# A decoder layer with 32 experts on one core: the second modulation fused in row form, its row tiles handled one by one, and a fourth split buffer for the first expert

## The reference, cut to what matters

```
mod = silu(c) @ w_ada + b_ada ; shift1, scale1, g1, shift2, scale2, g2 = split(mod)
mixed = (sigmoid(ga) * y_ret + sigmoid(gb) * y_fox) @ w_o
x = LN(1.189 * x + (1 + g1) * mixed) * ln1_w + ln1_b
h = x * (1 + scale2) + shift2
group = top1(softmax(h @ w_rg + b_rg)) ; experts = top2(in that group, h @ w_re + b_re)
y = sum over the 2 chosen experts of gate * ((silu(a) * u) @ w_e_out[e]),  a, u = split(h @ w_e_in[e])
x = LN(1.189 * x + (1 + g2) * y) * ln2_w + ln2_b
```

## Time and profile before

| | us |
|---|---|
| median of three runs (lowest, highest) | 1232.74 (1231.88, 1235.53) |
| the profiled execution, its own time | 1232.76 |
| its span, first to last instruction | 1230.9 |
| busy: PE, DVE, ACT, POOL | 1035.5, 877.7, 636.7, 260.7 |
| 566 to 607 us: PE busy, DVE busy, mean granted clock | 23.1, 27.7, 0.83 |
| 607 to 629 us: the same | 13.7, 17.8, 0.50 |
| 629 to 647 us: the same | 4.0, 10.3, 0.50 |
| 647 to 708 us: the same | 47.2, 48.1, 0.88 |

### The profile page before, as it was taken

How to read it: one execution, slowest core, us unless ns; L and a number is a source line. 1 busy time by engine, 2 the same in 40 slices (tenths; PEclk the granted TensorE clock), 3 DMA queues, 4 the chain that set the end, 5 groups by cost and what they waited for, 6 DMA issues and landing times.

```text
span 1230.9 us, 13075 instructions
## 1 busy us (share of the span) xinstructions
PE 1035.5 (84%) x4460; PEld 720.0 (58%) x4460; DVE 877.7 (71%) x944; ACT 636.7 (52%) x642; POOL 260.7 (21%) x192
## 2 busy tenths in 40 slices
PE   4698969899999999999247899999999999999950
PEld 2365647587777676677235556656665566556630
DVE  3868643396433444556766989999999999999947
ACT  3644414133323344523104677778777777777732
POOL 0240871010001000002807622111111122122210
PEclk8898988999999999999658999999999999999975
DMA  9777552255123324247126799999999999999923
GB/s 330 246 257 250 178 189 105 84 189 194 53 78 121 120 77 153 96 157 235 55 101 201 279 399 388 389 393 391 396 392 394 402 396 394 393 393 397 394 95 107
DMA packets 102666, 303.40 MB, mean 246 GB/s; under 512 B 10740, under 2 KB 10788, under 8 KB 102118
## 3 DMA queue, kind: packets, MB, share of 16 engines
q1 hardware_dynamic: 92888, 282.75, 61.7%
q0 software_dynamic: 9744, 20.19, 5.2%
HBM read 299.97 MB, written 14.73 MB: 256 GB/s over the span
## 4 chain that ended last, share of the span: by engine, by line
PE 60%; DVE 13%; POOL 10%; DMA 7%; ACT 5%; issue 4%; SPq 0%; ACTq 0%; POOLq 0%; DVEq 0%
PE banks L2025 10%; PE banks L1711 8%; PE banks L1722 8%; PE banks L2033 8%; PE banks L2021 7%; PE banks L1713 5%; DVE w_lo L1586 5%; ACT w_hi L972 4%; PE banks L2014 2%; DVE w_lo L1060 2%; DMA mod_sample<-scratch_mod 1%; PE banks L2040 1%; DMA w_raw<-in_w_ada 1%; DMA x_item<-scratch_h,slot_token 1%; POOL x L785 1%
## 5 line engine op out<-in xcount | busy, mean ns | idle before, releaser
L1586 DVE TENSOR_TENSOR w_lo<-w_raw,w_hi 128x2048 fp32r<-128x2048 f32 x157 | 360.2, 2311 | 38.5 <-ACT w_hi L972 38.5
L972 ACT ACTIVATE w_hi<-w_raw 128x2048 fp32r<-128x2048 f32 x157 | 295.6, 1903 | 0.9 <-PE banks L2025 0.7
L1060 DVE TENSOR_TENSOR w_lo<-w_raw,w_hi 128x2048 fp32r<-128x2048 f32 x72 | 165.7, 2319 | 79.6 <-ACT w_hi L811 79.4
L811 ACT ACTIVATE w_hi<-w_raw 128x2048 fp32r<-128x2048 f32 x72 | 136.8, 1910 | 140.3 <-PE banks L1722 110.4
L2025 PE MATMUL banks<-w_lo,xT_item 128*128 128x512 f32 x512 | 148.7, 412 | 47.1 <-DVE w_lo L1586 47.1
L2021 PE MATMUL banks<-w_hi,xT_item 128*128 128x512 f32 x512 | 157.4, 429 | 4.6 <-ACT w_hi L972 3.0
L2025 PEld LDWEIGHTS banks<-w_lo,xT_item 128*128 128x128 f32 x512 | 92.2, 190 | 92.9 <-DVE w_lo L1586 75.1
L1711 PE MATMUL banks<-w_hi,h_hi 128*128 128x512 f32 x384 | 142.6, 412 | 3.1 <-DVE gate_b L1098 1.4
L2021 PEld LDWEIGHTS banks<-w_hi,xT_item 128*128 128x128 f32 x512 | 94.7, 191 | 39.7 <-issue 14.4
L742 POOL DMA_INDIRECT scratch_y<-y_item,slot_row x29 | 63.9, 2204 | 226.0 <-DVE y_item L1610 209.0
L2033 PE MATMUL banks<-w_raw,hiddenT 128*128 128x512 f32 x248 | 111.4, 592 | 0.0
(11 more groups left out here) (427 smaller groups left out, 1488.5 us busy)
## 6 DMA issues: line engine op xcount, KB each, us to landing
w_raw<-in_w_e_in SPq DMA_DIRECT2D x128, 1024.0 KB, 7.2
w_raw<-in_w_e_out SPq DMA_DIRECT2D x64, 1024.0 KB, 5.8
w_raw<-in_w_in SPq DMA_DIRECT2D x32, 1024.0 KB, 8.9
w_raw<-in_w_ada SPq DMA_DIRECT2D x24, 1024.0 KB, 7.8
bias_rows<-in_b_in SPq DMA_DIRECT2D x16, 256.0 KB, 4.3
w_raw<-in_w_ret_proj SPq DMA_DIRECT2D x4, 1024.0 KB, 10.6
w_raw<-in_w_fox_proj SPq DMA_DIRECT2D x4, 1024.0 KB, 11.9
w_raw<-in_w_o SPq DMA_DIRECT2D x4, 1024.0 KB, 5.0
```

Of the source, the lines that this page charges most:

```text
L811: nc.scalar.activation(whi[n % NSPL][:], raw[n % NRAW][:], ACT.Copy).then_inc(hi_done, 1)
L972: nc.scalar.activation(whi[ss][:], raw[j][:], ACT.Copy).then_inc(hi_done, 1)
L1060: V.tensor_tensor(wlo[n % NSPL][:], raw[n % NRAW][:], whi[n % NSPL][:].bitcast(F32), ALU.subtract).then_inc(lo_done, 1)
L1586: V.tensor_tensor(wlo[ss][:], raw[j][:], whi[ss][:].bitcast(F32), ALU.subtract).then_inc(lo_done, 1)
```

## The change

Five things are changed.

1. The modulation. `ada6` and `ada7` (shift2) now stay in `mod_rows`. When `ada8` and `ada9` (scale2) are evacuated, three more instructions on 2 x 512 values form (1 + scale2) * ln1_b + shift2 and (1 + scale2) * ln1_w right there. Two broadcast loads of ln1's rows (`ln_rows`) are issued ahead. POOL writes the finished shift row to `scratch_mod` after `ada9`, and waits for that write (`t2_out`) before the second `rotary`, since this writes over `mod_rows`. The eight POOL instructions and two loads later on are gone.
2. LN1 and h. Each row tile has its own variance, deviation, and two instructions for h straight from x; the three are placed among the instructions of the second `evac_wo`. x itself stays unnormalised until the tail. ACT instead of DVE copies the lower 64 rows (`low_rows`). PE computes a tile's logits right after its transposes. The router's weights are loaded earlier.
3. The routing chain has one instruction for three in five places, and `lo(N0 + 2)` is moved behind the last one-hot product. The token index is released ahead of the row index.
4. Item 0's fourth piece has its own buffers (`xhi`, `xlo`) and is split on ACT between the copies of h, and on DVE after the routing chain. ACT and DVE take item 1's first piece in its old place.
5. POOL's six instructions on x among the first items are gone. DVE does LN1's affine part with six instructions of 1024 columns ahead of the tail's first combination. The four tail loads, now six, stand behind the third gather.

The core of the diff:

```diff
+    xhi = at("w_hi_first", [P, 4, 512], F32R, 65536)
+    xlo = at("w_lo_first", [P, 4, 512], F32R, 90112)
+    FIRST_FREE = (N0 + 2, N0 + 3, N0 + 1, E0 + 1, E0 + 2)
@@ gpsimd
-            pool.dma_start(scratch["mod"][:, 512 * (j - 4):512 * (j - 3)], mrow[:, j % 2, :]).then_inc(mod_out[j % 2], 16)
+            if j not in SHIFT2:
+                pool.dma_start(scratch["mod"][:, 512 * (j - 4):512 * (j - 3)], mrow[:, j % 2, :]).then_inc(mod_out[j % 2], 16)
+            if j == 9:
+                pool.dma_start(scratch["mod"][:, D:2 * D], mod[:, D:2 * D]).then_inc(t2_out, 16)
+                pool.wait_ge(t2_out, 16)
             if 8 <= j <= 10:
                 rotary(j - 8)
...
-        pool.wait_ge(m2_in, 32)
-        pool.wait_ge(ln_in, 32)
-        for m2, rows in ((m2p, P), (m2s, DEC)):
...
-        pool.wait_ge(evacuated, CI["wo0"] + 1)
+        pool.wait_ge(used, SI[("wo1", 0)] + 1)
...
         gather_item(1)
-
+        gather_item(2)
...
-        for t in range(3):
-            rows = P if t < 2 else DEC
-            st(nc.gpsimd.tensor_tensor(x1[0:rows, t, :], x1[0:rows, t, :], l1w[0:rows, :], ALU.mult))
-            st.settle()
-            st(nc.gpsimd.tensor_tensor(x1[0:rows, t, :], x1[0:rows, t, :], l1b[0:rows, :], ALU.add), x1_ready)
@@ vector
+        def modulated(t):
+            rows = P if t < 2 else DEC
+            xt, ht = x1[0:rows, t, :], h2[0:rows, t, :]
+            m2 = m2p if t < 2 else m2s
+            dve.wait_ge(ln_std, t + 1)
+            st(V.reciprocal(mv[:, t, 1:2], mv[:, t, 1:2]))
+            if t == 0:
+                dve.wait_ge(m2_in, 32)
+            st(V.scalar_tensor_tensor(ht, xt, mv[0:rows, t, 0:1], m2[0:rows, 1, :], ALU.subtract, ALU.mult))
+            st.settle()
+            st(V.scalar_tensor_tensor(ht, ht, mv[0:rows, t, 1:2], m2[0:rows, 0, :], ALU.mult, ALU.add), h2_ready)
...
+            st(V.scalar_tensor_tensor(srow[:], rows, 1.0, l1r[:, 1, half], ALU.add, ALU.mult))
+            st(V.scalar_tensor_tensor(rows, rows, 1.0, l1r[:, 0, half], ALU.add, ALU.mult))
+            st.settle()
+            st(V.tensor_tensor(shift, shift, srow[:], ALU.add), evacuated)
...
+        dve.wait_ge(used, N0)
+        dve.wait_ge(hi_done, N0 + 4)
+        V.tensor_tensor(xlo[:], raw[(N0 + 3) % NRAW][:], xhi[:].bitcast(F32), ALU.subtract).then_inc(lo_done, 1)
         x_low(0)
-        lo(N0 + 3)
+        item_lo(1, 0)
...
-        dve.wait_ge(tail_in, 64)
-        dve.wait_ge(x1_ready, 3)
+        dve.wait_ge(tail_in, 96)
+        for t in range(3):
+            rows = P if t < 2 else DEC
+            xt = x1[0:rows, t, :]
+            st(V.scalar_tensor_tensor(xt, xt, mv[0:rows, t, 0:1], l1w[0:rows, :], ALU.subtract, ALU.mult))
+            st.settle()
+            st(V.scalar_tensor_tensor(xt, xt, mv[0:rows, t, 1:2], l1b[0:rows, :], ALU.mult, ALU.add))
@@ tensor
-            if t:
-                logits(t - 1)
-        logits(2)
+            logits(t)
```

More of the change, by code:

```diff
@@ L1001, in item @@
         def item(e, second):
-            item_hi(e, 0)
+            if not (isinstance(e, int) and e == 1):
+                item_hi(e, 0)
             silu(e - 1)
@@ L1526, in _ @@
         st.settle()
[L1527 to L1528 removed]
+        st(V.tensor_tensor(oht6, oh6, exc[:, :].unsqueeze(1).to_broadcast([P, 6, NE]), ALU.mult))
         st.settle()
@@ L1617, in item_steps @@
         def item_steps(e, second, third):
-            item_lo(e, 0)
+            if not (isinstance(e, int) and e == 1):
+                item_lo(e, 0)
             hidden(e - 1)
@@ L2020, in product @@
                 for half in range(2):
-                    mm(bank[b0 + half], X[:, k0 + kk, :], whi[ss][:, 2 * kk + half, :], start=(first and kk == 0), stop=False)
+                    mm(bank[b0 + half], X[:, k0 + kk, :], split_h[ss][:, 2 * kk + half, :], start=(first and kk == 0), stop=False)
             pe.wait_ge(lo_done, n + 1)
@@ L2024, in product @@
                 for half in range(2):
-                    last = mm(bank[b0 + half], X[:, k0 + kk, :], wlo[ss][:, 2 * kk + half, :], start=False, stop=(final and kk == 1))
+                    last = mm(bank[b0 + half], X[:, k0 + kk, :], split_l[ss][:, 2 * kk + half, :], start=False, stop=(final and kk == 1))
             last.then_inc(used, 1)
```

208 lines of the change are left out of this document (112 added, 96 removed).

## The result

| | before | changed |
|---|---|---|
| median, us (lowest, highest) | 1233.39 (1231.88, 1235.53) | 1202.28 (1199.99, 1205.07) |
| the profiled execution, its span | 1230.9 | 1198.5 |

A second series gave 0.9748 (0.9714 to 0.9781).

A forecast was written before the change was run, and what follows sets the result against it. Compute was taken to pace the item loop, which the change leaves alone, so savings ahead of it are kept. The terms -13.1 - 1.5 - 11.1 + 6.7 + 3.2 = -15.8 us gave 1217.0 us, range 1210 to 1224.

The forecast's parts named there:

- The rotation: Ahead of the loop: POOL's wait for its write delays the second rotary and all queued behind; +6.7 us, bounds +4 and +9.
- The rotation's delay is covered: Rival, ahead of the loop: the rotation's 6.7 us vanish as ACT's small DMA might go faster; 1210.3 us, chance 0.07.
- the rotation's end doesn't move: Sign of being wrong, ahead of the loop: forecast had POOL's second rotation starting 5 us later.
- LN1 to the logits: Ahead of the loop, LN1 through h to the logits: read at 611.6 instead of 624.64; -13.1 us, bounds -11.5 to -16.
- The routing chain: Behind the logits: merged instructions, earlier index and moved lo save time; -1.5 us, bounds 0 and -2.5.
- The items: First items of the loop: without POOL's work on x they take the loop's period; -11.1 us, bounds -8 and -13.
- the slower rival: Item loop: it settles at a longer period, over 0.3% slower from +0.70 us a period; chance 0.03.
- The tail: After the loop: DVE's six instructions are covered but hold up the last hold and scatter; +3.2 us, bounds +1.1 and +7.9.
- The scatter is not held: Rival, tail: descriptor work goes on beside DVE, only the hold costs 1.1 us; 1214.9 us, chance 0.15.
- The tail is shut: Rival, tail: DVE leaves POOL no gap, hold and scatter run after it; +7.9 instead of +3.2, 1221.7 us, chance 0.15.

The follow-up runs named there:

- changed_again: The changed kernel once more, unedited, in one series with together_dve_first and early_dve_first; 1202.81 us, ratio 0.9748.
- before_again: The kernel before once more, unedited, for a second profile of its front part; 1234.61 us, ratio 0.9993.
- delay_only: The kernel before plus three dependent DVE instructions on 2 x 512 values behind ada9's evacuation, result unused; 1225.08 us, ratio 0.9912.
- fold_later: The changed kernel with the three instructions folding ada9's half into the shift rows behind rv0's pair of w_lo, POOL waiting for them; 1218.17 us, ratio 0.9872.
- no_wait: The changed kernel with the shift rows in a place of their own, so POOL does not wait for their write; 1199.40 us, ratio 0.9702.
- together_dve_first: all_together plus a wait: POOL starts its third rotation only after DVE has finished rv1's pair of w_lo; 1200.21 us, ratio 0.9735.
- all_together: The changed kernel with no_wait's rows, fold_later's fold, the two result DMAs behind the first rotation and tail_split's tail; 1200.53 us, ratio 0.9702.
- fourth_shared: The changed kernel with item 0's fourth piece back in its shared buffer, it and item 1's first piece split in their old places; 1203.70 us, ratio 0.9733.
- early_dve_first: The changed kernel with result DMAs behind the first rotation, tail_split's tail, and POOL's third rotation held until DVE finishes rv1's w_lo pair; 1194.79 us, ratio 0.9686.
- tail_split: The changed kernel with DVE's six LN1 affine instructions moved off the last hold and scatter, four before and two behind; 1199.89 us, ratio 0.9691.

## Why the prediction was wrong, step by step

The differences in us, by the first pair of profiles and by changed_again less before_again:

| stretch | forecast | first pair | second pair |
|---|---|---|---|
| up to the first `wo0` instruction | +6.7 | -10.3 | -6.7 |
| from there to the logits | -13.1 | -13.7 | -13.4 |
| logits to item 0's transposes | -1.5 | -0.7 | -0.9 |
| item 0's transposes to the last ones | -11.1 | -8.45 | -8.05 |
| the last transposes to the last `y_item` | 0 | -0.9 | 0.0 |
| last `y_item` to the first combination | +3.2 | +1.7 | +1.4 |
| sum | -15.8 | -32.4 | -27.7 |

**The rotation** is the step that failed, by 13 to 17 us, and two sentences of it. The first: "The six extra instructions on 2 x 512 values (2.2 us a chunk at 0.72) delay DVE and PE ahead of this wait, so they cost nothing; without the rotation's delay they would cost up to 1.5." They moved DVE's pair by 3.9 us (from 134.17 to 138.10), off POOL's fourth instruction; that saved POOL the 4.6 us which the wait then took (delay_only, fold_later). The second is that the transposes, the DMAs and ACT's wait are queued behind the rotation, so that its delay passes on whole, with PE at its transposes 0.57 us after the rotation's end. In the changed kernel the rotation ended 3.9 us earlier, mostly because POOL started its third tile ahead of DVE's pair of `w_lo`. PE came to its transposes 8.8 us after that end, at 177.19 instead of 172.90, since that pair took 10.04 us. But it did not stand there for 9.48 us. ACT's wait ends when the small DMA lands, and that was 5.8 us after its issue and not 8.2, with SP's 2 MB behind it. I had read the 17.16 us of the earlier trace rows and named the DMA in the rival "The rotation's delay is covered", but gave it 0.07 and a gain of 6.7 at most; a time ahead of the kernel before was in none of my cases. That rival's mechanism was close, loads that go faster, and its size was not. I had named as a sign of being wrong that the rotation's end doesn't move; it moved the other way. The size of the term was sound where its placement holds: in fold_later PE's products come 7.0 and 6.0 us later than in the two profiles of the kernel before, against +6.7.

Up to PE's first product behind the transposes this makes 6.3 us less in the first pair (181.72 against 187.99) and 5.8 in the second. What is added up to `wo0` is **PE's clock**. From that product to the first `wo0` instruction it is 389.1 us in both profiles of the kernel before, and 385.1 and 388.2 in the two of the changed one:

```profile
400.00:500.00 100.00, 97.07 (x504) 70.16 (x503) 47.80 (x98) 42.29 (x97) 1.26 (x2) 1.00 0.38 127
...
400.00:500.00 100.00, 96.37 (x487) 69.20 (x488) 48.54 (x97) 40.66 (x91) 1.26 (x2) 0.98 0.37 127
```

(The changed kernel's first profile, then changed_again; the last three columns are clock, DMA share and GB/s.) Two things are in it. The kernel before restarts PE at half clock after its 9.48 us of standing, 0.63 us a product instead of 0.40, which costs about 2.5 us. And every profile has a few short dips of the granted clock while PE is busy. In the item loop one can be priced: an item with a dip has 0.91 and takes 17.9 us, one at 1.00 takes 16.4, so a dip costs about 1.55 us. In this stretch, by the granted clock of pieces of 50 us, the changed kernel's first profile has none, the kernel before has one in both profiles (0.97 from 400 to 450 us), and changed_again has two (0.97 from 450 to 500 and from 500 to 563). So 385.1, plus 1.55 a dip, plus the restart, gives 389.15 for the kernel before and 388.2 for changed_again, as measured. The other profiles come out the same way: 388.2 with two dips in no_wait, together_dve_first and four others, 386.6 and 386.7 with one in all_together and fourth_shared, 385.2 with none in early_dve_first, and 386.4 in fold_later with none and a restart of 1.3 us. The restart is a gain of the change; how many dips fall in the stretch differs even between two executions of the same kernel, and no run shows what places them.

**LN1 to the logits**: right in mechanism and size, 13.4 to 13.7 against 13.1. **The routing chain**: from the logits to POOL's first gather it is 1.7 us less, but that gather's rows reach PE 1.0 us later, so 0.7 to 0.9 is left. Inside its bounds.

**The items**: right in mechanism and close in size. Items 2 to 4 are as forecast (16.51, 16.36 and 16.37 us). Item 1 takes 16.52 instead of my 15.4 because PE runs a part of it at half clock (granted clock 0.79 from 632.0 to 648.5): four matmuls take 2.07 us there, and 1.20 in no_wait, which has the same items' code:

```profile
642.46 2.07 PE L2063 MATMUL banks<-w_hi,xT_item 128*128 128x512 f32 x4
...
643.52 1.20 PE L2064 MATMUL banks<-w_hi,xT_item 128*128 128x512 f32 x4
```

In no_wait, fold_later, together_dve_first and early_dve_first item 1 has a clock of 1.00 and takes 15.33 to 15.38 us, and from item 1 to item 5 no_wait takes 64.6 us, 11.0 less than the kernel before. Some 1.5 of that are a dip in item 3 of the kernel before (17.91 us at 0.90), which I had put down to POOL's work. In the first pair 1.25 us more came back in the 27 items behind, since one of them took 17.94 us, a dip again. The loop kept its period of 16.4, so the slower rival fell. The 0.9 us of the first pair between the last transposes and the last `y_item` are of this kind too (a granted clock of 0.82 in the kernel before, 0.90 or 0.91 in the other three profiles).

**The tail**: half of the 3.2, with the mechanism I had. `hold` lost 0.98 (I had 1.1), the scatter 0.99 (I had 2.1: it got in after one instruction, not three). The rival "The scatter is not held" fell. The Trainium skill (SBUF — State Buffer, Who interferes with whom) infers that a DVE `tensor_tensor`, which takes only the read side of the shared pair, doesn't stop descriptor generation. The scatter took 1.89 us beside DVE instructions with SBUF inputs and 0.90 us without them in tail_split, and the loop's scatters took 2.20 us beside `w_lo`, which is a TENSOR_TENSOR, so the measurement decides against it for this DMA. Which part of the scatter's issue is held, the descriptors or the reading of its indices from SBUF, no run tells. "The tail is shut" fell too.

## What to carry to other kernels

Where two engines slow each other down, ask of every edit, even of one that costs nothing, which of them it makes first at the next meeting. Write down both orders, price each, and if one is much better, enforce it with a wait. When other engines wait for a small DMA, issue it as soon as its data exist; here that was worth 9 to 11 us. Give a term a range on both sides of zero when it rests on where two engines happen to meet. And before a difference of 1 to 3 us between two profiles is put down to an edit, compare the granted clock of that stretch: here dips of about 1.55 us came and went between executions of the same kernel.
